# Two-layer transformer kernel: expert weights in mixed gate/up units of two transfers each, two more places for them, another order of loading

## The reference, cut to what matters

```python
for e in range(N_EXPERTS):
    hid = jax.nn.silu(h @ w_gate[e]) * (h @ w_up[e])
    out = out + gate[..., e:e + 1] * (hid @ w_down[e])
...
ple = jax.nn.sigmoid(h @ ple_gate[i]) * (p[i] @ ple_proj[i])
h = layer_norm(DEEPNORM_ALPHA * h + ffn + ple, ln2_g[i], ln2_b[i])
```

## Time and profile before

| | |
|---|---|
| time of the profiled execution | 1781.88 us |
| its span | 1780.6 us |
| median of 3 runs | 1781.26 us |
| mean granted TensorE clock | 0.976 |
| PE busy | 1682.7 us (95%) |
| PEld, DVE, ACT, POOL busy | 74%, 49%, 40%, 5% |
| bytes read from HBM | 409.54 MB |

### The profile page before, as it was taken

The page is one execution under the profiler, slowest core; times in us unless marked ns, Lnnn a source line. Parts: engine busy times, 40 slices in busy tenths (PEclk is TensorE's granted clock), DMA queues, the critical chain, the costliest instruction groups (busy, mean ns, idle before and its releaser), DMA issues.

```text
span 1780.6 us, 25951 instructions
## 1 busy us (share of the span) xinstructions
PE 1682.7 (95%) x11072; PEld 1311.6 (74%) x11072; DVE 872.8 (49%) x1137; ACT 719.7 (40%) x1082; POOL 91.9 (5%) x152
## 2 busy tenths in 40 slices
PE   5899999997899999998799999999999999999998
PEld 4787844332887853443598899799989889989997
DVE  4786611001566711110564756655566475565555
ACT  3475411111457511111364544444446444444443
POOL 1000101100000111100001000000000100000000
PEclk9899999999899999999899999999999999999999
DMA  7434699999533689999663455465546436645552
GB/s 212 149 104 172 274 418 417 417 417 371 172 134 110 259 344 416 417 417 416 215 202 120 145 187 205 142 222 190 189 126 210 147 115 212 209 146 201 187 187 88
DMA packets 193111, 413.13 MB, mean 232 GB/s; under 512 B 16416, under 2 KB 130848, under 8 KB 176608
## 3 DMA queue, kind: packets, MB, share of 16 engines
q1 hardware_dynamic: 191904, 409.83, 63.8%
q10 hardware_dynamic: 1088, 1.57, 0.4%
HBM read 409.54 MB, written 1.84 MB: 231 GB/s over the span
## 4 chain that ended last, share of the span: by engine, by line
PE 80%; DMA 11%; DVE 6%; ACT 1%; issue 1%; POOL 0%; SPq 0%; DVEq 0%; ACTq 0%
PE PS L459 10%; PE PS L463 10%; PE PS L460 10%; PE PS L1557 9%; PE PS L467 8%; PE PS L470 8%; PE PS L471 8%; DMA weights_at_lo<-in_w_up 5%; PE PS L1579 3%; DMA weights_raw<-in_w_in 3%; DMA arena<-in_w_up 3%; PE PS L1532 2%; PE PS L486 2%; DVE weights_lo L439 2%; PE PS L1591 1%
## 5 line engine op out<-in xcount | busy, mean ns | idle before, releaser
L439 DVE TENSOR_TENSOR weights_lo<-weights_raw,weights_hi 128x1024 fp32r<-128x1024 f32 x368 | 431.6, 1216 | 219.8 <-ACT weights_hi L432 219.4
L459 PE MATMUL PS<-hT_hi,weights_hi 128*128 128x256 f32 (+1 forms) x1488 | 424.3, 285 | 16.4 <-ACT weights_hi L432 11.5
L432 ACT ACTIVATE weights_hi<-weights_raw 128x1024 fp32r<-128x1024 f32 x368 | 365.5, 1045 | 150.4 <-PE PS L471 73.3
L463 PE MATMUL PS<-hT_hi,weights_lo 128*128 128x256 f32 (+1 forms) x1488 | 421.6, 283 | 2.9 <-DVE weights_lo L439 2.9
L460 PE MATMUL PS<-hT_lo,weights_hi 128*128 128x256 f32 (+1 forms) x1488 | 421.4, 283 | 0.0
L459 PEld LDWEIGHTS PS<-hT_hi,weights_hi 128*128 128x128 f32 (+1 forms) x1488 | 283.5, 191 | 23.7 <-issue 19.8
L463 PEld LDWEIGHTS PS<-hT_hi,weights_lo 128*128 128x128 f32 (+1 forms) x1488 | 283.2, 190 | 4.9 <-DVE weights_lo L439 4.2
L460 PEld LDWEIGHTS PS<-hT_lo,weights_hi 128*128 128x128 f32 (+1 forms) x1488 | 283.5, 191 | 2.0
L467 PE MATMUL PS<-weights_hi,opa_hi 128*128 128x512 f32 x384 | 152.8, 398 | 1.3 <-DVE opa_lo L669 1.1
L470 PE MATMUL PS<-weights_lo,opa_hi 128*128 128x512 f32 x384 | 152.0, 396 | 0.0
L471 PE MATMUL PS<-weights_hi,opa_lo 128*128 128x512 f32 x384 | 151.9, 396 | 0.0
(11 more groups left out here) (319 smaller groups left out, 2377.7 us busy)
## 6 DMA issues: line engine op xcount, KB each, us to landing
weights_raw<-in_w_in SPq DMA_DIRECT2D x80, 1024.0 KB, 5.7
weights_raw<-in_w_ff SPq DMA_DIRECT2D x64, 1024.0 KB, 5.2
weights_raw<-in_w_up SPq DMA_DIRECT2D x18, 1024.0 KB, 15.4
arena<-in_w_down SPq DMA_DIRECT2D x18, 1024.0 KB, 20.3
weights_raw<-in_w_gate SPq DMA_DIRECT2D x16, 1024.0 KB, 21.4
weights_at_hi<-in_w_gate SPq DMA_DIRECT2D x16, 1024.0 KB, 20.6
weights_at_lo<-in_w_up SPq DMA_DIRECT2D x16, 1024.0 KB, 19.7
arena<-in_w_gate SPq DMA_DIRECT2D x14, 1024.0 KB, 21.2
```

Of the source, the lines that this page charges most:

```text
L432: act.activation(u.flat[0][:, c:e], u.x[:, c:e], ACT.Copy).then_inc(*sig.mark("w_hi", u.u, i))
L439: dve.tensor_tensor(u.flat[1][:, c:e], u.x[:, c:e], u.flat[0][:, c:e].bitcast(F32), ALU.subtract).then_inc(*sig.mark("w_lo", u.u, i))
L459: pe.matmul(o, w[0], x[0], start=start, stop=False)
L463: return pe.matmul(o, w[1], x[0], start=False, stop=stop)
```

## The change

- **Units.** The gate and up units become `wide e ic` (c = 0, 1): 4 rows of both, but only 256 columns of each, gate in the left half of the unit and up in the right. `load_unit` issues one transfer for each half. The pieces of a partition are now 1 KB long. A half of `gate_and_up` uses `wide e i0` and `wide e i1`, one for each half of the partitions.
- **Hidden values.** With gate and up of one slot side by side in the bank, silu (ScalarE, 128x256) and the product (VectorE, 128x256, one input in PSUM) come first, and two transposes turn the product only; ScalarE copies it.
- **0/1 matrices.** GpSimd does nothing more here. VectorE makes the columns of a group in two instructions and the rows of two experts in one, straight from PSUM. The spreading matmuls move from ahead of the first `pick` into the loop, one bank for two experts.
- **Places.** The 16 KB that held the spread numbers become two places, AT_LOW and AT_HIGH (15 places in all); like AT_A they wait for `mla y`.
- **Order of the list.** The first three units of an expert stand between `ple gate 0` and `ple gate 1` (N_EARLY = 3), the last four (down 14 and 15) behind the first dense unit of the next part (N_LATE = 4).
- **Smaller things.** `add_to_tokens` adds the high part of both tiles first, then the low part. The split of the next part's first dense unit is done one expert earlier. SP issues one dense unit less ahead of the flag.

```diff
         w = a["w_in"][l]
         if l > 0:
             cols("mla 0", w, 0)
+            plan += late
...
         rows("ple proj", a["ple_proj"][l], 0)
-        for i in range(4):
+        experts = expert_units(a, l)
+        cols("ple gate 0", a["ple_gate"][l], 0)
+        plan += experts[:N_EARLY]
+        for i in range(1, 4):
             cols(f"ple gate {i}", a["ple_gate"][l], 256 * i)
-
-        add_experts(plan, a, l)
+        plan += experts[N_EARLY:-N_LATE]
+        late = experts[-N_LATE:]
...
+        if l > 0:
+            cols("gla v0", w, GV)
+        else:
+            cols("gla v0", w, GV)
+            plan += late
+        cols("gla v1", w, GV + 256)
...
-def add_experts(plan, a, l):
+def expert_units(a, l):
+    found = []
     for e in range(N_EXP + 1):
         for i in range(2 if e < N_EXP else 0):
-            for n in ("gate", "up"):
-                w = a["w_" + n][l, e].rearrange("(p k) n -> p k n", p=P)
-                plan.append((f"{n} {e} {i} {l}", w[:, 4 * i:4 * i + 4, :], 4, 512))
+            both = [a["w_" + n][l, e].rearrange("(p k) n -> p k n", p=P)[:, 4 * i:4 * i + 4, :] for n in ("gate", "up")]
+            for c in range(2):
+                found.append((f"wide {e} {i}{c} {l}", tuple(w[:, :, 256 * c:256 * c + 256] for w in both), 4, 512))
         for i in range(2 if e > 0 else 0):
             w = a["w_down"][l, e - 1][256 * i:256 * i + 256, :]
-            plan.append((f"down {e - 1} {i} {l}", w.rearrange("(k p) n -> p k n", p=P), 2, D))
+            found.append((f"down {e - 1} {i} {l}", w.rearrange("(k p) n -> p k n", p=P), 2, D))
+    return found
...
-        N_PLACE = NRAW + 2 * NSPLIT + 4
-        AT_A, AT_PARAMS, AT_PLE, AT_GAINED = range(N_PLACE - 4, N_PLACE)
+            return name.startswith(("wide ", "down "))
+
+        N_PLACE = NRAW + 2 * NSPLIT + 6
+        AT_A, AT_LOW, AT_HIGH, AT_PARAMS, AT_PLE, AT_GAINED = range(N_PLACE - 6, N_PLACE)
+        IN_ARENA = (AT_A, AT_LOW, AT_HIGH, AT_PLE, AT_GAINED)
...
                 if left == 0:
-                    left = 6 * N_EXP
-                    free_from[AT_A], free_from[AT_PARAMS], free_from[AT_GAINED], free_from[AT_PLE] = -1, u - 4.5, u - 4.4, u + 0.5
-                    held[AT_A] = held[AT_PARAMS] = held[AT_GAINED] = held[AT_PLE] = None
+                    left, v = 6 * N_EXP, place[f"ple gate 3 {name[-1]}"] + 1
+                    for i, at in ((AT_A, -1), (AT_LOW, -1), (AT_HIGH, -1), (AT_PARAMS, v - 4.5), (AT_GAINED, v - 4.4),
+                                  (AT_PLE, v + 0.5)):
+                        held[i], free_from[i] = None, at
+                d = before_experts[int(name[-1])] % NSPLIT
                 allowed = [i for i in range(N_PLACE) if (left > 12 or i != AT_PARAMS) and
-                           (left > 12 or (i in (AT_A, AT_PLE, AT_GAINED)) == (left <= 3))]
+                           (left > 10 or i not in (NRAW + d, NRAW + NSPLIT + d)) and
+                           (left > 12 or (i in IN_ARENA) == (left <= len(IN_ARENA)))]
                 at = min(allowed, key=lambda i: free_from[i])
                 found.append((at, held[at], None, None))
                 held[at], free_from[at] = u, u
                 left -= 1
...
             elif u.raw >= AT_A:
                 l = int(u.name[-1])
-                sp.wait_ge(*(sig.at("ps", f"mla y {l}"), sig.at("norm_dve", f"ln1 {l} new1"),
-                             sig.at("moe_dve", f"h and ple {l}"), sig.at("norm_dve", f"ln1 {l} new1"))[u.raw - AT_A])
-            sp.dma_start(u.whole, plan[u.u][1]).then_inc(*sig.landing(f"raw{u.raw}_loaded", u.u))
+                sp.wait_ge(*{AT_A: sig.at("ps", f"mla y {l}"), AT_LOW: sig.at("ps", f"mla y {l}"),
+                             AT_HIGH: sig.at("ps", f"mla y {l}"), AT_PARAMS: sig.at("norm_dve", f"ln1 {l} new1"),
+                             AT_PLE: sig.at("moe_dve", f"h and ple {l}"),
+                             AT_GAINED: sig.at("norm_dve", f"ln1 {l} new1")}[u.raw])
+            src = plan[u.u][1]
+            if isinstance(src, tuple):
+                for i, part in enumerate(src):
+                    sp.dma_start(u.whole[:, :, 256 * i:256 * i + 256], part).then_inc(*sig.landing(f"raw{u.raw}_loaded", u.u))
+            else:
+                sp.dma_start(u.whole, src).then_inc(*sig.landing(f"raw{u.raw}_loaded", u.u))
...
-        gate_up = [mem(9216 + 512 * i, 512) for i in range(2)]
+        hid_rows = [mem(9216 + 256 * i, 256) for i in range(2)]
         hid_e = [mem(10240 + 256 * i, 256).rearrange("p (k s) -> p k s", k=4) for i in range(2)]
-        sil = mem(10752, 256).rearrange("p (k s) -> p k s", k=4)
+        sil = [mem(9728 + 256 * i, 256) for i in range(2)]
...
+            def turn_slots():
+                b = banks.take(pe, n_("slot T"), "dve_took", among=4)
+                for t in range(NT):
+                    last = transpose(pe, PS[0:16, b, t * P:(t + 1) * P], slot[:, t, :])
+                last.then_inc(*sig.mark("ps", n_("slot T")))
...
             def gate_and_up(e_, i):
 
                 if i == 0:
-                    banks.take(pe, n_(f"gate up {e_}"), "act_took", among=4)
+                    banks.take(pe, n_(f"gate up {e_}"), "dve_took", among=4)
                 b = banks.of(n_(f"gate up {e_}"))
-                if e_ % GROUP == i == 0:
-                    pe.wait_ge(*sig.at("act_took", n_(f"pick {e_ // GROUP} 2")))
-                    pe.wait_ge(*sig.at("dve_took", n_(f"pick {e_ // GROUP} 3")))
-                w = [loaded(pe, n_(f"{which} {e_} {i}")) for which in ("gate", "up")]
+                if e_ % GROUP == 0:
+                    pe.wait_ge(*sig.at("act_took", n_(f"pick {e_ // GROUP} {2 * i}")))
+                    pe.wait_ge(*sig.at("dve_took", n_(f"pick {e_ // GROUP} {2 * i + 1}")))
+                w = [loaded(pe, n_(f"wide {e_} {i}{j}")) for j in range(2)]
                 for k in range(4):
                     x = x_e[e_ // GROUP % 2][:, 4 * i + k, e_ % GROUP, :]
                     for j in range(2):
                         last = pe.matmul(PS[SLOTS * j:SLOTS * j + SLOTS, b, :], x, w[j][:, k, :], start=i == k == 0,
                                          stop=i == 1 and k == 3)
-                last.then_inc(*sig.mark("ps", n_(f"gate {e_} {i}")))
-                sig.also("ps", n_(f"up {e_} {i}"))
+                last.then_inc(*sig.mark("ps", n_(f"wide {e_} {i}0")))
+                sig.also("ps", n_(f"wide {e_} {i}1"))
...
             def turn_hidden(e_):
 
-                b = banks.take(pe, n_(f"turn {e_}"), "dve_took", among=4)
-                pe.wait_ge(*sig.at("act_took", n_(f"gate up {e_}")))
-                for c in range(4):
-                    last = transpose(pe, PS[:, b, c * P:(c + 1) * P], gate_up[e_ % 2][:, c * P:(c + 1) * P])
+                b = banks.take(pe, n_(f"turn {e_}"), "act_took", among=4)
+                pe.wait_ge(*sig.at("dve_took", n_(f"gate up {e_}")))
+                for f in range(2):
+                    last = transpose(pe, PS[:, b, f * P:(f + 1) * P], hid_rows[e_ % 2][:, f * P:(f + 1) * P])
...
-                pe.wait_ge(*sig.at("moe_pool", n_(f"rows {e_}")))
-                pe.wait_ge(*sig.at("dve_took", n_(f"down {e_}")))
-                for t in range(NT):
-                    for part in range(2):
+                pe.wait_ge(*sig.at("dve_took", n_(f"rows {e_ - e_ % 2}")))
+                for part in range(2):
+                    pe.wait_ge(*(sig.at("dve_took", n_(f"down {e_}")) if part else sig.at("moe_act", n_(f"down {e_}"))))
+                    for t in range(NT):
                         for half in range(2):
                             r = slice(SLOTS * half, SLOTS * half + SLOTS)
-                            last = pe.matmul(PS[:, 4 + 2 * t + half, :], from_slot[r, t * P:(t + 1) * P], y_e[part][r, e_ % 2, :],
-                                             start=e_ == 0 and part == 0, stop=e_ == N_EXP - 1 and part == 1)
-                    if t == 0 and e_ == N_EXP - 1:
-                        last.then_inc(*sig.mark("ps", n_("ln2") + " t0"))
+                            last = pe.matmul(PS[:, 4 + 2 * t + half, :], from_slot[r, e_ % 2, t * P:(t + 1) * P],
+                                             y_e[part][r, e_ % 2, :], start=e_ == 0 and part == 0,
+                                             stop=e_ == N_EXP - 1 and part == 1)
+                        if t == 0 and part == 1 and e_ == N_EXP - 1:
+                            last.then_inc(*sig.mark("ps", n_("ln2") + " t0"))
                 last.then_inc(*sig.mark("ps", n_(f"add {e_}")))
...
             pick(0)
+            turn_slots()
...
+                if e_ == 1:
+                    pe.wait_ge(*sig.at("dve_took", n_("slot T")))
+                if e_ % 2:
+                    spread(e_ - 1)
...
-            def take_gate_up(e_):
-                name = n_(f"gate up {e_}")
-                act.wait_ge(*sig.at("ps", n_(f"up {e_} 1")))
```

(87 more changed lines are left out.)

45 lines of the change are left out of this document (6 added, 39 removed).

## The result

The changed kernel takes 1875.8 us (median of 4 runs, 1872.7 to 1877.4) against 1780.8 for the kernel before (4 runs, 1776.4 to 1782.1): ratio 1.0536, with an interval from 1.0513 to 1.0559. It is 95 us slower; the forecast was 62 us, 1844, with a range up to 1872. So the direction was right and the time lies beyond the upper end.

A forecast was written before the change was run, and what follows sets the result against it. DMA transfers of expert units bound the kernel. Per layer, the longer transfer sum (+42.4 us), earlier start (-5.6) and shorter tail (-5.8) gave +31.0; both layers +62.0, so 1844 us, range 1808 to 1872.

The forecast's parts named there:

- The silence of SP: Start of experts: fourth unit waits for AT_A until about 214 us, so 3 units are ahead instead of 12.
- The start: First pick and first half of expert 0: done at 213.9 us, so SP may go on 5.6 us earlier.
- TensorE's wait between the halves of expert 0: Expert 0: TensorE waits a whole transfer for the fourth unit, idle some 5 us, hidden in the transfer sum.
- Rival 4: Experts: TensorE becomes the bound as waits lower its clock; a few us a layer more, 1845 to 1860; no chance given.
- At 376 a unit takes 2.79 us; I take that: Expert loads: a wide unit runs at the ple gate loads' 376 GB/s, 2.79 us each, 61 per layer.
- what a wide unit costs: Expert loads with 1 KB pieces: 2.79 us per unit, bounds 2.515 and 3.00 us.
- rival 2: Expert loads: wide units cost as much as w_in's, 3.00 us; +43.8 us per layer, 1870 us; chance 0.13.
- The tail: End of experts: layer norm starts 4.1 us after the last unit instead of 9.95; gain 5.8 us per layer.
- 5.8 - 3.0 of the sum: End of experts, per layer: 5.8 us gained behind the last unit, 3.0 us added by loading `mla 0 1` earlier.
- The early units in front of `ple gate 1`: Before the experts: ple gates 1 to 3 load later but in time by 4 to 5 us; costs nothing.
- What was called covered: Experts: transposes, silu, spreading and VectorE edits change TensorE's 13.46 us per expert by less than one; count nothing.
- Rival 1: Expert loads: shorter pieces cost nothing, 2.515 us per wide unit; +14.2 us per layer, 1810 us; chance 0.13.

The follow-up runs named there:

- The free place: Changed kernel, but places of the three early units count as used later, so following units take empty places first: 1815.6 us, ratio 1.0188.
- the halves in the kernel before: Kernel before, with only each gate and up unit loaded as two transfers of 256 columns (1 KB pieces): 1840.9 us, ratio 1.0334.

## Why the prediction was right, and where it was wrong

**The silence of SP: right, in place and time.** The arithmetic of `assign_places` said that the fourth unit would ask for AT_A. It did; SP was free at 214.22 us where 213.9 was forecast. The free place turned it into 60 us less. The start hardly missed. In the chain that ended last (start, length, what) the pick takes 3.83 + 1.05 us, the transposes 0.32, and the first half 3.67:

```profile
204.88 3.83 PE PS L1557 x32
208.71 1.05 PE PS L1566 x32
209.75 0.32 PE PS L511 x2
210.07 0.47 issue
210.54 3.67 PE PS L1582 x16
```

**TensorE's wait between the halves of expert 0: right, 5.5 us.** The timeline of TensorE has it at 219.66 us, and a second one behind it; the granted clock of 214 to 225 us is 0.69:

```profile
219.66 5.56 PE L1582 MATMUL PS<-arena,picked 128*64 128x512 f32 x16 [5.46 <-DMA arena<-in_w_up]
226.55 0.62 PE L1582 MATMUL PS<-weights_raw,picked 128*64 128x512 f32 x1 [1.33 <-DMA arena<-in_w_up]
```

The half takes 5.56 us instead of 3.67, and still costs nothing, since the transfers set the pace. Rival 4 did not come in: the clock is down to 0.94 and 0.93 in the plateau, but TensorE still has idle time there and DMA's share stays at 1.08, so the slow stretches use up waits that are there anyway.

**"At 376 a unit takes 2.79 us; I take that": this step failed.** The term "what a wide unit costs" was too small. A wide unit measured 3.00 to 3.05 us, which is rival 2 (3.00, chance 0.13), and 0.26 us, 122 times, are the whole of the missing 32 us (with the 1.8 us per layer of the down units in it). The prediction had both rows before it and chose by likeness of the rows' pitch: ple gates are regular, w_in starts at odd offsets. What mattered was that the ple gate stretches were 2 us out of a single load into an idle queue, and w_in's lay within 7 us of a full one. The windows of the trace after show the turn, where three wide units and three ple gates, all of 1 KB pieces, follow one another:

```profile
164.00:165.50 1.50, 1.50 (x8) 1.23 (x7) 0.00 (x0) 0.79 (x1) 0.00 (x0) 1.00 1.08 379
165.50:167.00 1.50, 1.50 (x8) 1.20 (x7) 1.20 (x2) 1.22 (x2) 0.00 (x0) 1.00 1.02 335
167.00:168.50 1.50, 1.50 (x8) 1.21 (x7) 1.50 (x3) 0.00 (x0) 0.00 (x0) 1.00 1.04 348
168.50:170.00 1.50, 1.50 (x8) 1.23 (x7) 1.35 (x4) 0.42 (x1) 0.00 (x0) 1.00 1.10 364
170.00:171.50 1.50, 1.50 (x8) 1.18 (x8) 1.01 (x2) 0.83 (x2) 0.41 (x1) 1.00 1.10 350
...
176.00:177.50 1.50, 1.50 (x12) 1.36 (x12) 0.87 (x2) 0.84 (x2) 0.55 (x1) 1.00 1.10 347
177.50:179.00 1.50, 1.50 (x15) 1.50 (x14) 1.41 (x2) 0.00 (x0) 0.01 (x1) 1.00 1.10 346
179.00:180.50 1.50, 1.50 (x18) 1.50 (x17) 0.00 (x0) 0.50 (x2) 0.00 (x0) 1.00 1.10 347
```

The first unit shows 379 GB/s soon after its start, as a ple gate by itself does; then the rate moves between 335 and 364, and the ple gates at the end of the train, the same transfers from the same tensor, hold 346 to 347. Part of the difference is where the window lies. The load at 571 us in the trace before moves at 160 GB/s from 570 to 571 us, at 377 and 384, and at 128 from 573 to 574: the earlier trace rows has its fast middle without its slow ends. Taken whole (stretch times DMA share), three single loads in that trace keep the engines busy for 3.06 to 3.24 us, against 3.01 x 1.10 = 3.31 for a unit in the train and 2.79 x 1.09 = 3.04 by the 2 us window. Why a single load is still somewhat cheaper was not tried and stays open; that the offsets of w_in's rows were no reason is shown, since rows without them cost as much. With the stretch of w_in as the price the sum is the prediction's own 1870, 6 us below the measured time; 3 to 4 of these are the down units at 2.57 instead of 2.515 us.

The range failed with the same step. Its upper end was 1872, while rival 2 stood at 1870 with 3.00 us as "the upper bound" of a unit; but 349 GB/s over 7 us was a single reading, not a bound, and nothing was left above it for the other terms.

**The tail: right.** 4.06 us behind the last unit, 4.1 forecast. The net of the moved end is smaller (1.7 us) than the 5.8 - 3.0 of the sum, since without it the norm follows 7.97 us behind and not 9.95.

**The early units in front of `ple gate 1`: right, nothing.** The splits of the ple gates begin when they did.

**What was called covered: right.** The edits of the arithmetic left TensorE's pace as it was, 53.79 against 53.83 us, with what the transposes give and what the spreading takes in balance. The "0.3 us per expert" for the transposes is nearer 0.2 by their busy time (0.8 us in four experts). A small part was missed behind the norm: the layer's next parameters are issued 508.00 - 493.88 = 14.1 us behind its start, where it was 13.2 before, 0.9 us.

**Rival 1 (pieces cost nothing): refuted** by the halves in the kernel before, which cost 60 us with nothing changed but the transfers. The Trainium skill ("DMA: Bandwidth & Descriptors", Specifications) has 512 B as the size from which a transfer runs at line rate. By that rule the plateau would have stayed at 417; here 1 KB pieces hold 348 in a train, and even 4 KB pieces lengthen a unit by 3% (2.56 against 2.49 us). The same page of the Trainium skill (Why small descriptors are slow (HBM only)) tells of a fixed overhead of about 3 cycles per packet beside beats of 32 B. The form, a fixed price for each piece, is what the table above shows. The size is not: an estimate from these two figures of the Trainium skill makes 35 cycles of 1 KB and 259 of 8 KB, 8% longer for the same bytes. The unit measured 3.00 against 2.49 us, 21%.

## What to carry to other kernels

When the price of a transfer is read from a trace, read it in the middle of a long train of transfers, as they will run in the new place; 2 us out of a single load flatter. Where two rows disagree on a price that is multiplied by 122, the choice between them is the forecast, and the range should reach beyond the worse one.

A rule that hands out buffers by "longest free in list order" is part of the schedule: who walks through its arithmetic finds a silence of 33 us (181 to 214) before it happens, and one line repairs it. Gate and up side by side in a unit saved TensorE 0.2 us of transposes per expert and cost each of its four wide units 0.5 us of transfer; where the layout in memory can be chosen, one contiguous run for each partition keeps the first without the second.

## What the runs showed of the hardware

- Each contiguous piece in memory adds a fixed price, about 0.57 ns of the time of a full queue over 16 DMA engines, the same from 4 KB down to 1 KB within the rounding: 417, 409, 394 and 367 GB/s in the plateau as its wide units go from 8 to 4, 2 and 1 KB, and 348 where only 1 KB pieces are in the queue.
- A single load of 1 MB in pieces of 1 KB shows 376 to 380 GB/s in the 2 us of its middle; in a train the first 7 us had 335 to 379, and from then on it was 346 to 350.
- Down units, with pieces of 4 KB, moved at 408 GB/s between wide units at 348.
- Neither a second transfer of 512 KB for each unit nor a destination in 1 KB pieces adds to it what can be told from noise: one transfer into one contiguous run took 1873.5 us (1872.2 to 1876.6), two into interleaved columns 1875.8 (1872.7 to 1877.4).
- DMA's busy share does not tell a good plateau from a bad one: it was 1.02 at 417 GB/s and 1.08 at 367. The rate does.
